# Moving the memory's second key and value projection from the GLA stage to RWKV's second half

## The reference

```python
mem_n = rms_norm(mem, mem_norm_g)
for layer in range(DEPTH):
    xn = rms_norm(h, norm_mix_g[layer])
    if layer % 2 == 0:
        proj = xn @ ab_w_in[j]
        y_a = gla_group(proj[..., :GLA_COLS], ...)
        y_b = rwkv7_group(proj[..., GLA_COLS:], ...)
...
def memory_cross_attention(xn, mem_n, wq, wkv, wo):
    q = (xn @ wq).reshape(B, T, XA_HEADS, XA_DH)
    kv = (mem_n @ wkv).reshape(B, M, 2, XA_HEADS, XA_DH)
```

## Time and profile before

| | us |
|---|---|
| median of 3 runs | 3203.3 (3201.73 to 3204.18) |
| the profiled execution | 3200.58 |
| its span, first to last instruction | 3198.8 |
| mean granted TensorE clock | 0.985 |

### The profile page before, as it was taken

How to read it: one execution, slowest core, us unless ns; L and a number is a source line. 1 busy time by engine, 2 the same in 40 slices (tenths; PEclk the granted TensorE clock), 3 DMA queues, 4 the chain that set the end, 5 groups by cost and what they waited for, 6 DMA issues and landing times.

```text
span 3198.8 us, 38637 instructions
## 1 busy us (share of the span) xinstructions
PE 3072.7 (96%) x16592; PEld 2443.3 (76%) x16592; DVE 1570.7 (49%) x1919; ACT 1178.4 (37%) x1532; POOL 141.9 (4%) x154
## 2 busy tenths in 40 slices
PE   8999898999999999999999998999999999999999
PEld 6897676778887667778887774688887888778887
DVE  6444455555543765555443745633336443553333
ACT  5433432433322564433322545522224333342221
POOL 1010000000000100000000200000000000000000
PEclk9999999999999989999999999999999999999999
DMA  4362001223332311223332330133323222233331
GB/s 154 112 198 60 15 28 41 92 66 92 96 96 76 100 53 66 92 66 93 105 86 76 90 99 27 40 105 92 92 93 102 84 95 83 79 86 99 92 96 62
DMA packets 350490, 270.51 MB, mean 85 GB/s; under 512 B 28672, under 2 KB 331264, under 8 KB 350064
## 3 DMA queue, kind: packets, MB, share of 16 engines
q1 hardware_dynamic: 346384, 252.83, 26.4%
q0 software_dynamic: 3936, 15.22, 1.4%
HBM read 261.73 MB, written 6.29 MB: 84 GB/s over the span
## 4 chain that ended last, share of the span: by engine, by line
PE 84%; DVE 8%; ACT 5%; issue 1%; POOL 0%; DMA 0%; DVEq 0%; SPq 0%; ACTq 0%; POOLq 0%
PE ps L189 84%; ACT arena L203 2%; DVE arena L220 2%; ACT whi L206 1%; DVE arena L212 1%; DVE wlo L212 1%; DVE hT L212 1%; PE ps L192 1%; DVE xlo L220 1%; ACT L203 1%; DVE sml L229 0%; DVE xlo L212 0%; POOL arena L212 0%; DVE arena L216 0%; ACT arena L206 0%
## 5 line engine op out<-in xcount | busy, mean ns | idle before, releaser
L189 PE MATMUL ps<-xhi,whi 128*128 128x512 f32 (+2 forms) x2192 | 874.7, 399 | 12.8 <-DVE xlo L212 5.7
L189 PE MATMUL ps<-split,whi 128*128 128x512 f32 (+2 forms) x2640 | 833.8, 393 | 28.1 <-DVE hT L212 19.8
L189 PE MATMUL ps<-xhi,wlo 128*128 128x512 f32 (+2 forms) x2192 | 857.4, 391 | 0.0
L189 PE MATMUL ps<-xlo,whi 128*128 128x512 f32 (+2 forms) x2192 | 857.3, 391 | 0.0
L212 DVE TENSOR_TENSOR wlo<-wraw,whi 128x2048 fp32r<-128x2048 f32 (+4 forms) x258 | 550.7, 2137 | 505.6 <-ACT whi L206 505.5
L189 PEld LDWEIGHTS ps<-split,whi 128*128 128x128 f32 (+1 forms) x2640 | 491.2, 189 | 157.5 <-issue 30.9
L206 ACT ACTIVATE whi<-wraw 128x2048 fp32r<-128x2048 f32 (+4 forms) x258 | 456.1, 1771 | 359.4 <-PE ps L189 349.4
L189 PE MATMUL ps<-split,wlo 128*128 128x512 f32 (+2 forms) x1320 | 510.3, 387 | 0.0
L189 PEld LDWEIGHTS ps<-xhi,whi 128*128 128x128 f32 (+2 forms) x2192 | 410.5, 187 | 122.2 <-issue 11.6
L189 PEld LDWEIGHTS ps<-xhi,wlo 128*128 128x128 f32 (+2 forms) x2192 | 410.8, 187 | 91.0 <-issue 5.3
L189 PEld LDWEIGHTS ps<-xlo,whi 128*128 128x128 f32 (+2 forms) x2192 | 410.3, 187 | 91.0
(11 more groups left out here) (115 smaller groups left out, 1928.1 us busy)
## 6 DMA issues: line engine op xcount, KB each, us to landing
wraw<-in_ffn_w_up SPq DMA_DIRECT2D x128, 512.0 KB, 5.2
wraw<-in_ffn_w_down SPq DMA_DIRECT2D x32, 1024.0 KB, 5.1
wraw<-in_odd_w_in SPq DMA_DIRECT2D x24, 1024.0 KB, 5.1
wraw<-in_ffn_w_gate SPq DMA_DIRECT2D x44, 512.0 KB, 4.0
wraw<-in_xattn_wkv SPq DMA_DIRECT2D x16, 1024.0 KB, 5.4
wraw<-in_xattn_wq SPq DMA_DIRECT2D x8, 1024.0 KB, 5.2
wraw<-in_xattn_wo SPq DMA_DIRECT2D x8, 1024.0 KB, 5.1
wraw<-in_cd_w_in SPq DMA_DIRECT2D x8, 1024.0 KB, 5.4
```

Of the source, the lines that this page charges most:

```text
L189: return self.e.matmul(out, lhsT, rhs, start=start, stop=stop, skip_group_check=True)
```

## The change

`Memory` is made for one layer, with its own source operand. GLA computes layer 0 only. Once the memory is split, GpSimd copies the whole operand (128x4096, 2 MB) from the arena to a DRAM tensor `mem_scratch`. In RWKV, when the last projection has read `xs`, GpSimd loads it back into `xhi`; layer 1's 16 blocks are computed from there in the dense stream on bank 7, one a step, and staged for their store in the last 512 columns of `xlo`. To make room for the 16 steps, output products 0, 1 and 2 issue two blocks a step, four steps each; both blocks of a step use bank 7. Product 3's additions wait for the last store. Cross attention 1 reads what RWKV's memory stage stored.

```diff
+        kept = nc.dram_tensor("mem_scratch", (P, 4096), F32R, kind="Internal").ap()
...
-            def __init__(self, S, st, made, of):
+            def __init__(self, S, l, src, st, made, of):
...
-                for ku, vu in self.layers:
-                    yield from fm_tensor(pe, self.S, ku, mem, self.made, 256, of=self.of)
-                    yield from tm_tensor(pe, self.S, vu, mem, self.made, of=self.of)
+                yield from fm_tensor(pe, self.S, self.keys, self.src, self.made, 256, of=self.of)
+                yield from tm_tensor(pe, self.S, self.values, self.src, self.made, of=self.of)
...
-            memory = Memory(S, sent, lambda k: S.V.of("mem_lo", k), range(6, 8))
+            memory = Memory(S, 0, mem, sent, lambda k: S.V.of("mem_lo", k), range(6, 8))
+            S.l_kept = landing("mem_kept")
...
+                pool.wait_ge(S.A.of("mem_hi", 7), S.V.of("mem_lo", 7))
+                pool.dma(kept, split[:, 0:4096]).then_inc(*S.l_kept.up("x", by=16))
                 for _ in memory.gpsimd(pool):
...
+            l_back = landing("mem_back")
+            mem2 = [Src(xhi[:, k * 512:k * 512 + 256], xhi[:, k * 512 + 256:k * 512 + 512]) for k in range(8)]
+            S.memory = memory = Memory(S, 1, mem2, [xl[:, 3584:3840], xl[:, 3840:4096]], lambda k: l_back.of("x"), of_dense)
...
+            def twos(g):
+
+                for _ in g:
+                    next(g, None)
+                    yield
...
-                    yield from steps(8, out(q, 0))
-                    yield from steps(8, out(q, 1))
-                    yield from steps(12, out(q, 2))
+                    yield from steps(4, twos(out(q, 0)))
+                    yield from steps(4, twos(out(q, 1)))
+                    yield from steps(2, iter(()))
+                    yield from steps(16, blocks(q))
+                    yield from steps(4, twos(out(q, 2)))
                     yield from out(q, 3)
...
+            def last_vector(dve, p):
+                if p == 3:
+                    dve.wait_ge(*memory.ends())
+                yield from add_vector(dve, S, outs[p], carry if p == 3 else None)
...
+                pool.wait_ge(S.P.of("rkv3", 2), l_kept.of("x"))
+                pool.dma(xhi, kept).then_inc(*l_back.up("x", by=16))
+                for _ in memory.gpsimd(pool):
+                    pass
                 carry.gpsimd(pool)
...
-        then(lambda S: xattn(1, S.ends, S.carry, ("norm_ffn_g", 1), s_gla[0].memory))
+        then(lambda S: xattn(1, S.ends, S.carry, ("norm_ffn_g", 1), s_rwkv[0].memory))
```

More of the change, by code:

```diff
@@ L835, in build @@
         class Memory:
-            def __init__(self, S, st, made, of):
[L839 to L850, removed]
+            def __init__(self, S, l, src, st, made, of):
+                self.S, self.src, self.st, self.made, self.of = S, src, st, made, of
+                self.sent = [landing(f"kv{l}_sent0"), landing(f"kv{l}_sent1")]
+                wkv = D["xattn_wkv"][l]
+                self.keys = fm_units(f"key{l}", 1024, [(wkv[:, 0:1024], 0)])
+                self.values = tm_units(f"value{l}", wkv, 1024, 1024, 2)
+                self.out = [(u[0], key, kvd[l][:, key[1] * 256:(key[1] + 1) * 256])
+                            for u in self.keys for key, _, _ in u[3]]
+                self.out += [(u[0], key, kvd[l][:, 2048 + key[1] * 1024 + key[2] * 256:2304 + key[1] * 1024 + key[2] * 256])
+                             for u in self.values for key, _ in u[3]]
             def tensor(self, pe):
-                for ku, vu in self.layers:
-                    yield from fm_tensor(pe, self.S, ku, mem, self.made, 256, of=self.of)
-                    yield from tm_tensor(pe, self.S, vu, mem, self.made, of=self.of)
+                yield from fm_tensor(pe, self.S, self.keys, self.src, self.made, 256, of=self.of)
+                yield from tm_tensor(pe, self.S, self.values, self.src, self.made, of=self.of)
             def vector(self, dve):
@@ L1546, in gla, with rwkv @@
             return S, tensor, vector, scalar, gpsimd, None
-        def rwkv(ends, nxt):
+        def rwkv(ends, nxt, l_kept):
             S = Stage("rwkv", sem)
@@ L1591, in steps, with streams @@
                     raise ValueError("too many steps")
-            def streams(q, features, heads, tail, project, out):
+            def twos(g):
+                for _ in g:
+                    next(g, None)
+                    yield
+            def streams(q, features, heads, tail, project, out, blocks):
                 def chain(c):
@@ L1632, in tensor @@
                         lambda q, p: add_tensor(q, S, outs[p], [ys[p % 2]], [P], lambda k: S.V.of("ys", p),
-                                                of=range(8) if p == 3 else of_dense))
+                                                of=range(8) if p == 3 else of_dense), memory.tensor)
             def turned(pe, key, src, event):
@@ L1850, in vector @@
                 streams(dve, features_vector, heads_vector, tail_vector, project_vector,
-                        lambda q, p: add_vector(q, S, outs[p], carry if p == 3 else None))
+                        last_vector, memory.vector)
+            def last_vector(dve, p):
+                if p == 3:
+                    dve.wait_ge(*memory.ends())
+                yield from add_vector(dve, S, outs[p], carry if p == 3 else None)
             def project_vector(dve, p):
@@ L2009, in scalar @@
                 streams(act, features_scalar, heads_scalar, tail_scalar, project_scalar,
-                        lambda q, p: add_scalar(q, S, outs[p], carry=carry if p == 3 else None))
+                        lambda q, p: add_scalar(q, S, outs[p], carry=carry if p == 3 else None), memory.scalar)
             def project_scalar(act, p):
@@ L3484, in build @@
         s_gla = gla(first[0].ends, first[0])
-        s_rwkv = rwkv(lambda: s_gla[0].ends() + s_gla[0].memory.ends(), ("norm_xattn_g", 0))
+        s_rwkv = rwkv(lambda: s_gla[0].ends() + s_gla[0].memory.ends() + [s_gla[0].l_kept.end()], ("norm_xattn_g", 0),
+                      s_gla[0].l_kept)
         stages = [first, s_gla, s_rwkv]
```

## The result

| | before | changed |
|---|---|---|
| median, us | 3202.8 (3201.7 to 3204.2, 4 runs) | 3229.9 (3224.3 to 3231.4, 4 runs) |
| the profiled execution | 3200.6 | 3231.4 |
| its span | 3198.8 | 3229.6 |
| mean granted TensorE clock | 0.985 | 0.979 |

The ratio is 1.0081, with a 95% interval of 1.0069 to 1.0094: the change costs 27.1 us by the medians, 30.8 between the two profiled executions. In what follows, sums are made between the profiled ones, as in the prediction.

A forecast was written before the change was run, and what follows sets the result against it. TensorE, busy 96% of the span, was taken as the bound. Terms -45.6 + 32.2 + 25.0 - 1.8 + 9.7 + 1.1 + 2.0 gave +22.6 us: 3223.2 profiled, median 3226, range 3209 to 3240.

The forecast's parts named there:

- GLA: GLA stage: losing the memory's 16 second-layer blocks saves 45.6 us, with the junction to the output product costed at nothing.
- rival 5: GLA's output product: weights can't keep up with its earlier start, 5 to 8 us come back, 3232; chance 0.05.
- The two transfers: GpSimd's queue: two more 2 MB transfers cost 0, bounds 0 and 8.1 us.
- Rounds 52 to 67: RWKV's second half: one memory block a round makes 76.9 us of today's 44.7, so +32.2.
- Rival 3: Rounds 52 to 67: idle time of weight loads is room, 64.8 us instead of 76.9, total 3214; chance 0.14.
- The pairs in rounds 42 to 49: RWKV, products 0 and 1: second blocks wait 20.3 us for additions, eight more blocks take 7.2; +25.0 in all.
- the old 2.77: Round 47: TensorE's existing 2.77 us wait for four operations in VectorE's own order was to stay.
- Rivals 1 and 2: Pairs' waits: nothing, 3194, chance 0.05 (first); about half, within 0.2% of before, 3206, chance 0.08 (second).
- the clock term: TensorE at half clock after added waits: one or two more stretches, +2 us, bounds 0 and 6.
- Rival 4: Rounds 42 to 49 and 68 to 71: mostly half clock, some 12 us more, 3238; chance 0.15.
- every 1.73 us: Product 2 in pairs, rounds 68 to 71: blocks were to follow each other at this one-bank cycle.
- The late conversion: After product 3 begins: next stage's unit is converted 4.4 us after that start instead of 3.3, so +1.1.

## Why the prediction was right

**GLA** gave 45.4 of the 45.6. The output product follows the last block directly, 22.70 of 23.52 us busy, so the 4.2 for an uncovered conversion didn't arise, and rival 5 fell.

**The two transfers** landed in 7.7 and 8.2 us (DMA issues: tensor, queue, count, KB, us to landing), and the first memory block, at 485.32, follows the chain without a wait. Cost 0, as taken.

```profile
mem_scratch<-split POOLq DMA_DIRECT2D x1, 2048.0 KB, 7.7
...
xhi<-mem_scratch POOLq DMA_DIRECT2D x1, 2048.0 KB, 8.2
```

**Rounds 52 to 67**: 76.0 us against 76.9 worked out. All waits of the earlier trace rows in this stretch are gone, the conversions cost nothing, and the waits for a copy are 0.21 to 0.30 where 0.3 was taken.

**Rival 3** wanted 64.8 us for the same stretch, since weight loads were busy 28.0 us where matmuls showed 39.0. The 12 us of room did not appear: matmuls are now busy 74.67 of 76.01 us with loads at 68.00, and the stretch lasted as long as its matmuls in a row. The Trainium skill, page "Perfetto Trace Analysis", section "Identifying the Most-Contended Engine", says to judge headroom by the share of peak arithmetic or of the weight loads, not by matmul busy time. By this trace, in this stretch of small matmuls taken in order, matmul busy time was the better measure.

**The pairs in rounds 42 to 49**, waits: 0.78, 4.46, 3.21, 0.78, 5.71, 0.78, 1.75, 0.87 measured against 1.0, 4.5, 3.4, 0.9, 6.3, 0.9, 1.9, 1.4. The walk through the two engines' orders gave 20.3, the trace 18.3; the mechanism, the place and the order of size of each wait were right, and the old 2.77 stayed, as said. Two kernels show the cause: with a second bank all eight vanish and rounds 42 to 49 are 19.4 us shorter, and with the pairs alone these rounds are 27.4 longer and the kernel 31. Rivals 1 and 2 fell with that.

**What failed is the clock term**: +2 taken, with bounds of 0 and 6, and about 13 measured. In rounds 42 to 49 TensorE is busy 43.15 - 29.37 = 13.8 us more. Eight blocks at 0.9 are 7.2 of it; the other 6.6 is the same work at 1.2 GHz, in five stretches of 30.6 us together where the kernel before had two of 6.8. Product 2 adds 4.7, the difference to the kernel with extra matmuls, and the stretch at 636.4 some 1.6. By the step of the prediction, "with 20 us more of waits I take one or two more", the waits were counted and the clock was priced as if one such stretch answered a wait here and there; in fact each of the three waits above 3 us ran into such a stretch, and so did those of 1.87 and 1.75. The trace of the kernel before already said more than the one stretch that was counted. The clock of 0.91 over rounds 42 to 49 is two of them: a second follows the wait of 2.77, and one of twice the length follows the wait of 5.22 (table of stretches, kernel before):

```profile
482.58:486.00 3.42, 3.42 (x35) 2.67 (x35) 0.82 (x2) 1.06 (x2) 0.00 (x0) 0.50 0.00 0
547.43:554.26 6.83, 4.93 (x12) 3.90 (x13) 4.81 (x6) 3.47 (x4) 0.00 (x0) 0.50 0.05 7
```

Of its five waits from 1.78 to 5.22 us from round 42 on, three were followed by half clock and two (1.87 and 2.49) were not. Rival 4 described what came: 6.6 and 4.7 us of lost clock in the two places that it names, where it had 12, in rounds 42 to 49 for less than half of the time and in product 2 for nearly all of it. The sum came out 8.2 below the measured 30.8: some 11 more for the clock, 2 less for the waits, 0.9 less for rounds 52 to 67, and small differences. By the profiled executions the changed kernel took 3231.4 us, and that is nearer to rival 4 (3238, less the same 2.7: 3235) than to the forecast (3223.2). Against the medians the miss is only 3.9, and that is luck: the forecast put the median 2.7 above the profiled execution, as it was before, and it came out 1.5 below it, which hid half of the miss.

**Product 2**: the sign "every 1.73 us" failed; the cycle was 2.43 at half clock and 1.74 with the clock restored. The first pair waited 0.56 and 1.77 with its conversion, so its second block starts 3.3 us after the last chain matmul, against 3.6 worked out.

**The late conversion**: cross attention 0 loses 1.7 us at its start, against 1.1. The other 1.6 of its +3.2 is clock.

## What to carry to other kernels

Before two steps of a stream are put into one, look at what frees the resource they share: here two blocks on one PSUM bank turned a read of 0.7 us by another engine into a wait of up to 5.7, with everything else queued behind it, while with a second bank the second blocks didn't wait at all. When waits are added, price the clock with them. And a move that fills idle time is worth at most that idle time, 17.5 us here, less what the moved work costs more in its new place and less the waits that open behind it.

## What the runs showed of the hardware

**The clock can stay down through waits of 0.78 us.** In the changed kernel's product 2 it fell to 1.2 GHz after the waits of 0.56 and 1.77 and stayed there for 20.5 us, though TensorE was busy 15.59 of them: 1.64 us of matmuls, then a wait of 0.78, six times over. With the waits filled to almost nothing the same blocks ran at 2.4 GHz throughout. Waits of this length are not enough by themselves, though. In the kernel with the pairs alone, product 2's blocks follow waits of 0.78, 0.52, 0.78, 0.52 and 0.78 us, with chain matmuls of 0.33 us between some, and TensorE is busy for a smaller share of the time; yet the clock, which had been at 1.2 GHz just before, is 1.00 all along:

```profile
550.80:554.20 3.40, 3.40 (x45) 2.66 (x46) 0.82 (x2) 0.00 (x0) 0.00 (x0) 0.50 0.88 298
554.30:567.80 13.50, 8.81 (x98) 5.41 (x92) 5.60 (x12) 0.00 (x0) 0.00 (x0) 1.00 0.01 3
```

What tells the two apart stays open.

**The same wait doesn't always cost the clock.** The wait of 1.87 us in round 42 precedes a stretch at half clock in the changed kernel; in the kernel with product 2 on all banks, whose program is the same up to there, the same 1.87 is followed by full clock. The stretches, of the changed kernel and of the other:

```profile
414.50:417.90 3.40, 3.33 (x5) 1.48 (x5) 1.26 (x2) 2.18 (x3) 0.00 (x0) 0.50 0.77 302
```
```profile
414.00:417.40 3.40, 2.42 (x8) 1.34 (x8) 1.82 (x2) 3.10 (x4) 0.00 (x0) 1.00 0.79 301
```

Both have the memory's load in flight, at 302 and 301 GB/s, so the transfer is not what tells them apart. What does stays open. It makes a price in clock uncertain by a stretch or two even where every wait is known; a stretch of 3.4 us that TensorE is busy throughout costs half of that, 1.7 us.

**The start of RWKV scatters.** It lies between 193.6 and 197.0 us in kernels whose instructions up to there are the same. Part of it is again the clock: the five kernels that reach it at 196.2 us or later show one or two half-clock stretches of 3.4 us in GLA or before it, and the other five, at 194.9 or earlier, none. From 34.9 us on, for one, the clock is 0.50 in the kernel with product 2 on all banks and 1.00 in the changed kernel. So a difference of two or three microseconds between two profiled executions, and the steps of the best kernels from one another, say less than the medians do.
